# A sample's outer product behind the next block's low parts, in a one-core retention stage

## The chip, the cores and the metric

The kernel runs on one core of one Trainium2 chip. The metric is device microseconds of the whole program on that core; each time is the median of several runs. The engines are named PE (TensorE, matrix products), DVE (VectorE), ACT (ScalarE), POOL (GpSimd) and SP (SyncE, which only issues transfers here). Each engine works through its own queue of instructions in order, and waits in that queue for semaphores that other engines raise.

## What is computed

The reference is one inference step of a two-layer decoder for 1024 new tokens and for 8 running samples of one token each: layer 1 is sliding-window attention and a ConvFFN, layer 2 is retention and a ConvFFN. The change touches the retention layer alone. What matters of it:

```
def step(s, inp):                      # one chunk of 128 tokens, one head
    inner = (q k^T) * decay_in
    o = inner v + (q s) * q_decay
    s = s * chunk_decay + (k * k_decay)^T v
    return s, o
...
mixer over the prompt:  s0 = 0, chunks of 128     (4 heads, keys 256 wide, values 512 wide)
mixer over the samples: s0 = state_ret, chunks of 1
out = (silu(g) * normalised o) @ w_o
```

For a sample the chunk is one token, so per head its state is decayed, gets the outer product of its key and its value, is multiplied by its query, and is written out. All products are float32.

## The kernel before

Every float32 operand of a product is split into a high and a low part, and each product is made as three PE products (high by high, low by high, high by low). ACT writes the high parts (names ending in h) and DVE or POOL subtracts them for the low parts (names ending in l). So weights go from a slab `raw` to `wh` (ACT, L1431) and `wl` (DVE, L2084), a block's keys to `r_kdh` (ACT, L1899) and `r_kdl` (DVE, L2722), its values to `r_vh` and `r_vl`, the state to `r_sh` (ACT, L1969) and `r_sl` (POOL, L3099).

The retention stage is written as `period(i)` for i = 0 to 33, one function of that name for each engine, so that each engine's order is the order of the lines of its own `period`. The 32 blocks are 4 heads times 8 chunks of 128 tokens (n is the chunk in its head); periods 32 and 33 only finish work. In PE's `period` stand, in order: fill 0, `inner` (L1315, keys times queries, waits for r_kdl), `back` of the block before, `update` 0, fill 1, `update` 1 (L792 with r_vh and r_kdh, the state's increment; it waits until DVE has taken update 0's increment into r_state, L2745), fill 2, `output` (the products with r_sh and r_sl), `turn` of the next block (transposes), fill 3, `sample_out`, fill 4. The fills are halves of jobs of the projection that makes the last head's operands (periods 0 to 15, two jobs each; jobs of kinds 1 and 3 are rotated on DVE, L2615, tile p_prod, the others copied on ACT, L1786, tile p_plain), and from 16 on four or five jobs of the output projection, whose results DVE adds to y (L2114). They keep PE busy while the other engines split and normalise.

DVE's `period` has, in order: `decayed` (r_inn, L2727), `gated` (r_ob), `update` 0 into r_state, `inner_lo`, fill 1, `update` 1, sums and masks of the samples, the first planned weight split, `outer`, fill 2, `norm`, `rows` of the next block (r_vl and r_kdl), split 2, fill 3, split 3, fill 4, split 4. The planned splits are a table: in block 12, for example, the third (with wh on ACT and wl on DVE at the same places); from block 16 on also the second.

Beside each block one state of a sample is worked through: SP loads the state (`sample_state`, r_s, 512 KB) and the sample's value row (`sample_values`, r_vb), ACT decays the state (`decay`, L1929), DVE adds the outer product (`outer`, L2755, two instructions of 128 x 512, both inputs in SBUF), PE multiplies it (`sample_out`, L1362), ACT writes it to memory (`sample_state_out`, L1941). Two states fit at a time. At the end `sample_back` (L1370) turns the samples' result.

Before period 0, ACT ends its `ret_pairs` with four plain copies of projection jobs (`LEAD` = 4, p_plain), each of which also issues a transfer; then come `queries_hi(0)` and `values_hi(0)` (r_qkh, r_vh, r_kdh of block 0).

```
dve.wait_ge(R["decay"], i + 1)
dve.wait_ge(R["vb"], 16 * i + 16)
for j in range(2):
    dve.scalar_tensor_tensor(K.s0[:, i % 2, j, :], K.vb[:, :], K.k16[:, j, i % NB:i % NB + 1], K.s0[:, i % 2, j, :],
                             ALU.mult, ALU.add).then_inc(R["outer"], 1)
```

Of the kernel before, what the change touches and what calls it, by code (L numbers as in the profile page):

```python
# [25 lines left out]
RH = 4  # L26
# [14 lines left out]
NI = RH * NB  # L41
# [81 lines left out]
LEAD = 4  # L123


def last_head_jobs():

    return ([(j, ch) for ch in range(NCH) for j in range(4, 8)] + [(2 * p + e, ch) for p in range(2) for ch in range(NCH) for e in range(2)]
            + [(j, ch) for j in (8, 9) for ch in range(NCH)] + [(j, ch) for ch in range(NCH) for j in (10, 11)])
# [668 lines left out]
def tensor_engine(pe, K):  # L798
# [486 lines left out]
    def fill(i, s):  # L1285

        if i < MIXED:
            if s < 4:
                ret_half(FILL[i][s // 2 * 2 + 1][0], s % 2)
            return  # L1290
        for key in FILL[i][s]:
            ret_out(key)
# [34 lines left out]
    def update(i, j):  # L1327
        pe.wait_ge(R["k_lo"], i + 1)
        pe.wait_ge(R["v_lo"], i + 1)
        after(pe, R["state"], 2 * i + j)  # L1330
        kk = slice(j * W, (j + 1) * W)
        accumulate(pe, kvB[:, :], [(K.kdh[:, kk], K.kdl[:, kk], K.vh[:, :], K.vl[:, :])]).then_inc(R["kv"], 1)
# [40 lines left out]
    def period(i):  # L1373
        h, n = divmod(i, NB)
        live = i < NI
        fill(i, 0)
        if live:
            inner(i)
        if 1 <= i <= NI:
            back(i - 1)  # L1380
        if live:
            update(i, 0)
        fill(i, 1)
        if live:
            update(i, 1)
            if n == 0:
                rows(h)
        if i in SAMPLES_BACK:
            sample_back(SAMPLES_BACK.index(i))
        fill(i, 2)  # L1390
        if live:
            output(i)
        if i + 1 < NI:
            turn(i + 1)
        fill(i, 3)
        if 1 <= i <= NI:
            sample_out(i - 1)
        fill(i, 4)

    for g in range(NG):  # L1400
# [9 lines left out]
def scalar_engine(act, K):  # L1410
# [468 lines left out]
    def ret_pairs(u):  # L1879
        ret_batch(u)  # L1880
        ffn_pair(RET, BATCH)
        for t in range(BATCH + 1, END_T[RET]):
            ret_pair(t)
        act.wait_ge(S["hq0"], START["hq0"] + out_count(END_T[RET] - 2))
        for j, ch in last_head_jobs()[:LEAD]:
            project(RH - 1, j, ch)
        for e in range(2):
            act.wait_ge(S[f"hp{e}"], START[f"hp{e}"] + 16 * PAIR_BASE[1] // 2)
# [86 lines left out]
    def fill(jobs):  # L1975
        for key in jobs:
            if key[0] == "p":
                project(*key[1:])

    def period(i):  # L1980
        h, n = divmod(i, NB)
        live = i < NI
        fill(FILL[i][0])
        if live:
            inner_hi(i)
        if 1 <= i <= NI:
            gated_out(i - 1)
        if n == 1 and h:
            sample_parts(h - 1)
        if i == NI + 1:  # L1990
            sample_root(RH - 1)
        fill(FILL[i][1])
        if live:
            decay(i)
            if n == 0:
                sample_rows(h)
        if i in HEADS_SPLIT[:-1]:
            heads_hi(HEADS_SPLIT.index(i))
        if i < NI:
            split_planned(i, 1)  # L2000
        elif FILL[i][1]:
            split_upto(J[FILL[i][1][-1]], U_F1)
        fill(FILL[i][2])
        if 1 <= i <= NI:
            sample_state_out(i - 1)
        if n == 2 and h and live:
            sample_root(h - 1)
        if i in SAMPLES_PUT:
            sample_put(SAMPLES_PUT.index(i))
        if i == HEADS_SPLIT[-1]:  # L2010
            heads_hi(len(HEADS_SPLIT) - 1)
        if live and n == NB - 1:
            state_out(h)
        if i + 1 < NI:
            queries_hi(i + 1)
        if live:
            heads_root(i)
        if i + 1 < NI:
            values_hi(i + 1)
        if live and n < NB - 1:  # L2020
            state_hi(i)
        if MIXED <= i < NI:
            split_planned(i, 2)
        fill(FILL[i][3])
        if i < NI:
            split_planned(i, 3)
        fill(FILL[i][4])
        if i < NI:
            split_planned(i, 4)
        elif FILL[i][4]:  # L2030
            split_upto(J[FILL[i][4][-1]], U_F1)
        if i == NI + 1:
            split_upto(J[FILL[i][3][-1]], U_F1 + 2)
# [13 lines left out]
    ret_pairs(3)  # L2047
    queries_hi(0)
    values_hi(0)
    for i in range(NI + 2):  # L2050
        period(i)
    last_chunks(6)
# [18 lines left out]
def vector_engine(dve, K):  # L2071
# [763 lines left out]
    def period(i):  # L2835
        h, n = divmod(i, NB)
        live = i < NI
        if i == NI + 1:
            sample_sums(RH - 1)
            sample_norm(RH - 1)  # L2840
        fill(FILL[i][0])
        if live:
            decayed(i)
        if 1 <= i <= NI:
            gated(i - 1)
        if live:
            update(i, 0)
            inner_lo(i)
        if i == NI + 1:
            sample_norm_rest(RH - 1)  # L2850
        fill(FILL[i][1])
        if live:
            update(i, 1)
        if n == 1 and live:
            if h:
                sample_sums(h - 1)
            masks(h)
        if n == 2 and h and live:
            sample_norm(h - 1)
        if i < NI:  # L2860
            split_planned(i, 1)
        elif FILL[i][1]:
            split_upto(J[FILL[i][1][-1]], U_F1)
        if 1 <= i <= NI:
            outer(i - 1)
        if i in SAMPLES_BACK:
            sample_gated(SAMPLES_BACK.index(i))
        fill(FILL[i][2])
        if n == 2 and h and live:
            sample_norm_rest(h - 1)  # L2870
        if live:
            norm(i)
        if i in SAMPLES_PUT:
            sample_put(SAMPLES_PUT.index(i))
        if i == NI + 1:
            last_heads_lo()
        if live:
            norm_rest(i)
        if i + 1 < NI:
            rows(i + 1)  # L2880
        if MIXED <= i < NI:
            split_planned(i, 2)
        fill(FILL[i][3])
        if i < NI:
            split_planned(i, 3)
        fill(FILL[i][4])
        if i < NI:
            split_planned(i, 4)
        elif FILL[i][4]:
            split_upto(J[FILL[i][4][-1]], U_F1)  # L2890
        if i == NI + 1:
            split_upto(J[FILL[i][3][-1]], U_F1 + 2)
# [272 lines left out]
def sync_engine(sp, K):  # L3165
# [193 lines left out]
    def period(i):  # L3359
        h, n = divmod(i, NB)  # L3360
        live = i < NI
        if i == 16:
            sp.wait_ge(S["jobs"], J["p", 3, 11, 2])
            heads(0, 2)
        if 1 <= i <= NI:
            slabs_to(planned_slabs(i - 1, 4) + RAW)
        elif i:
            slabs_to(min(due_by(J[(FILL[i - 1][4] or FILL[i - 1][3])[-1]]), S_F1) + RAW)
        if live:
            gates(i)  # L3370
        if i == 14:
            heads_written(8)
            sp.wait_ge(S["jobs"], J["p", 3, 11, 0])
            heads(0, 0)
        if n == 3 and h + 1 < RH:
            decays(h + 1)
        if i < NI:
            slabs_to(planned_slabs(i, 1) + RAW)
        elif FILL[i][1]:
            slabs_to(min(due_by(J[FILL[i][1][-1]]), S_F1) + RAW)  # L3380
        if i in (18, 19, 20):
            heads_written(16)
            heads_landed(i - 18, 1)
            heads(1, i - 18)
        if i == 23:
            heads_written(16 + 3)
            sp.wait_ge(S["jobs"], J["o", 0, 23])
            heads_landed(0, 2)
            heads(2, 0)
        if i == 25:  # L3390
            heads_written(16 + 6)
            heads_landed(1, 2)
            heads(2, 1)
        if i == 26:
            heads_written(24)
            heads_landed(2, 2)
            heads(2, 2)
        if i == 30:
            heads_written(24 + 3)
            sp.wait_ge(S["jobs"], J["o", 1, 23])  # L3400
            heads_landed(0, 3)
            heads(3, 0)
        if i == 31:
            heads_written(24 + 6)
            heads_landed(1, 3)
            heads(3, 1)
        if i == 33:
            heads_written(NI)
            heads_landed(2, 3)
            heads(3, 2)  # L3410
        if i + 1 < NI:
            sample_state(i + 1)
        if live:
            sample_values(i)
        if i == 15:
            sp.wait_ge(S["jobs"], J["p", 3, 11, 1])
            heads(0, 1)
        if i + 2 < NI:
            queries(i + 2)
            values(i + 2)  # L3420
# [206 lines left out]
```

## Time and profile before

| | us |
|---|---|
| median of 3 runs | 2732.18 (2731.06 to 2734.85) |
| the profiled execution | 2737.35 |
| its span in the trace | 2735.3 |
| PE busy in the span | 2665.0 (97%) |
| DVE busy | 1780.3 (65%) |
| ACT busy | 1095.6 (40%) |
| POOL busy | 764.1 (28%) |

The span is what the trace shows from the first instruction to the last; the execution's own time is 2 us longer. The retention blocks run from about 1484 to 1973 us of the span. Busy times are sums over an engine's instructions, so that a wait shows as the rest. In a row of the timeline, the bracket at the end gives how long the engine had been idle before the instruction, and what ended that.

### The profile page before, as it was taken

The page shows a single profiled execution, that of the slowest core. Times are in us where ns is not written, and L with a number is a line of the kernel's source. Part 1 is how long each engine was busy: PE and PEld are TensorE (multiplying, and loading weights), DVE is VectorE, ACT ScalarE, POOL GpSimd, SP SyncE. Part 2 cuts the span into 40 slices and gives each one's busy share as a digit, 9 for nine tenths or more (in the row PEclk, how much of TensorE's full clock was granted, in tenths as well). Part 3 has the DMA queues.
Part 4 walks back from the last instruction along what each step waited for, and adds up shares of the span by engine and source line. Part 5 has one row for each costly group of instructions (what it writes and reads, how often), then busy time and mean ns, then how long its engine had stood idle before and what let it go on. Part 6 is the DMA issues. An engine that isn't in the chain of part 4 may idle for free.

```text
span 2735.3 us, 48829 instructions
## 1 busy us (share of the span) xinstructions
PE 2665.0 (97%) x19550; PEld 2554.2 (93%) x19550; DVE 1780.3 (65%) x3272; ACT 1095.6 (40%) x2089; POOL 764.1 (28%) x601
## 2 busy tenths in 40 slices
PE   8999989999999999999999999999999999999997
PEld 7888879999999999999999888898899999999997
DVE  6556579676667445766463675777787766766455
ACT  5445446434433122633333435433264344342123
POOL 3344351322320002354250232333342223220021
PEclk9999999999999999999999999999999999999999
DMA  4210101222224232122324777776602221223321
GB/s 141 82 47 12 40 33 47 78 86 78 71 91 157 63 123 65 62 98 103 115 94 166 221 226 226 235 227 192 188 25 70 86 78 70 89 94 125 112 73 62
DMA packets 182576, 290.83 MB, mean 106 GB/s; under 512 B 24976, under 2 KB 131088, under 8 KB 182320
## 3 DMA queue, kind: packets, MB, share of 16 engines
q1 hardware_dynamic: 152112, 251.65, 28.4%
q10 hardware_dynamic: 30240, 36.07, 3.7%
q8 instruction: 156, 2.56, 0.4%
q14 instruction: 68, 0.56, 0.1%
HBM read 206.82 MB, written 82.93 MB: 106 GB/s over the span
## 4 chain that ended last, share of the span: by engine, by line
PE 84%; DVE 7%; issue 3%; ACT 2%; DMA 2%; POOL 2%; ACTq 0%; SPq 0%; POOLq 0%; DVEq 0%
PE bank L1085 13%; PE bank L1087 13%; PE bank L1086 13%; PE bank L792 12%; PE bank L794 12%; PE bank L793 12%; PE bank L825 2%; PE bank L827 2%; PE bank L826 2%; PE bank L946 1%; PE bank L925 1%; DVE r_s L2755 1%; DVE wl L2084 1%; ACT wh L1431 1%; PE bank L936 1%
## 5 line engine op out<-in xcount | busy, mean ns | idle before, releaser
L2084 DVE TENSOR_TENSOR wl<-raw,wh 128x512 fp32r<-128x512 f32 (+1 forms) x460 | 428.1, 934 | 310.5 <-ACT wh L1431 307.3
L1431 ACT ACTIVATE wh<-raw 128x512 fp32r<-128x512 f32 (+1 forms) x492 | 344.2, 714 | 405.8 <-PE bank L794 220.8
L1085 PE MATMUL bank<-xh,wh 128*128 128x258 f32 x1792 | 506.2, 283 | 0.0
L1087 PE MATMUL bank<-xh,wl 128*128 128x258 f32 x1792 | 505.7, 282 | 0.0
L1086 PE MATMUL bank<-xl,wh 128*128 128x258 f32 x1792 | 505.0, 282 | 0.0
L1086 PEld LDWEIGHTS bank<-xl,wh 128*128 128x128 f32 x1792 | 338.4, 189 | 0.0
L1085 PEld LDWEIGHTS bank<-xh,wh 128*128 128x128 f32 x1792 | 337.9, 189 | 0.0
L1087 PEld LDWEIGHTS bank<-xh,wl 128*128 128x128 f32 x1792 | 337.6, 188 | 0.0
L2116 DVE TENSOR_TENSOR y<-bank,y 128x344 f32<-128x344 f32 x384 | 191.7, 512 | 213.4 <-PE bank L794 212.5
L3034 POOL TENSOR_TENSOR raw<-raw 128x512 f32<-128x512 f32 x56 | 72.1, 1288 | 742.8 <-DVE wl L2084 742.5
L1085 PE MATMUL bank<-x_t2h,wh 128*128 128x258 f32 x896 | 253.1, 283 | 2.0 <-ACT f_ab L1658 2.0
L1086 PE MATMUL bank<-x_t2l,wh 128*128 128x258 f32 x896 | 253.0, 282 | 0.0
L1087 PE MATMUL bank<-x_t2h,wl 128*128 128x258 f32 x896 | 252.5, 282 | 0.0
L1658 ACT ACTIVATE f_ab<-bank 128x258 f32<-128x258 f32 x224 | 86.3, 386 | 270.7 <-PE bank L1087 267.9
L1085 PEld LDWEIGHTS bank<-x_t2h,wh 128*128 128x128 f32 x896 | 168.9, 189 | 2.3 <-DVE wl L2084 2.3
L1087 PEld LDWEIGHTS bank<-x_t2h,wl 128*128 128x128 f32 x896 | 169.3, 189 | 0.0
L1086 PEld LDWEIGHTS bank<-x_t2l,wh 128*128 128x128 f32 x896 | 169.2, 189 | 0.0
L792 PE MATMUL bank<-xh,wh 128*128 128x344 f32 x488 | 162.7, 333 | 2.4 <-DVE f_cv L2395 1.5
L825 PE MATMUL bank<-xh,wh 128*128 128x344 f32 x472 | 156.9, 332 | 2.6 <-DVE xl L2153 2.3
L794 PE MATMUL bank<-xh,wl 128*128 128x344 f32 x488 | 156.9, 321 | 0.0
L793 PE MATMUL bank<-xl,wh 128*128 128x344 f32 x488 | 156.8, 321 | 0.0
L1658 ACT ACTIVATE f_g<-bank 128x258 f32<-128x258 f32 x224 | 84.3, 380 | 179.4 <-PE bank L1087 179.4
(309 smaller groups left out, 7195.4 us busy)
## 6 DMA issues: line engine op xcount, KB each, us to landing
raw<-in_w SPq DMA_DIRECT2D x216, 512.0 KB, 3.8
scratch_h<-f_g SPq DMA_DIRECT2D x40, 516.0 KB, 2.7
h_in<-scratch_h SPq DMA_DIRECT2D x30, 688.0 KB, 5.0
r_s<-in_state_in SPq DMA_DIRECT2D x32, 512.0 KB, 3.8
out_state_s<-r_s ACTq DMA_DIRECT2D x32, 512.0 KB, 3.5
scratch_qkvg<-f_ab SPq DMA_DIRECT2D x16, 516.0 KB, 4.5
scratch_qkvg<-f_g SPq DMA_DIRECT2D x16, 516.0 KB, 5.5
r_cxq<-scratch_qkvg SPq DMA_DIRECT2D x32, 256.0 KB, 5.3
```

The source lines that it names most:

```text
L792: pe.matmul(out, ah, bh, start=(k == 0), stop=False)
L793: pe.matmul(out, ah, bl, start=False, stop=False)
L794: mm = pe.matmul(out, al, bh, start=False, stop=(k == n - 1))
L825: pe.matmul(out, ah, xh[:, k, c], start=(k == 0), stop=False)
L1085: pe.matmul(out, hi[:, kk], bh, start=(k == 0 and not adds), stop=False, skip_group_check=adds)
L1086: pe.matmul(out, hi[:, kk], bl, start=False, stop=False, skip_group_check=adds)
L1087: mm = pe.matmul(out, lo[:, kk], bh, start=False, stop=(k == 3), skip_group_check=adds)
L1431: act.activation(hi, source, ACT.Copy).then_inc(S["hi_done"], 1)
L1658: act.activation(out, bank[PRODUCT_BANKS[sub][n]][:, 0:TQ], ACT.Copy).then_inc(S[f"copied{sub}"], 1)
L2084: dve.tensor_tensor(lo, source, hi.bitcast(F32), ALU.subtract).then_inc(S["lo_done"], 1)
L2116: dve.tensor_tensor(t, bank[b][:, 0:CH], t, ALU.add).then_inc(S["yadd"], 1)
L3034: pool.tensor_tensor(g[:, two], g[:, one], g[:, two], ALU.add).then_inc(S["w_sum"], 1)
```

## The change

It moves work; nothing is computed otherwise.

- DVE: `outer` of the block before goes from the middle of the period (ahead of fill 2 and `norm`) to behind `rows` of the next block, ahead of split 2 and fill 3; with it the sums and masks of a head's samples.
- PE: `sample_out` goes from between fill 3 and fill 4 to the next period, behind fill 1 and ahead of `update` 1.
- ACT: `decay` is that of the block before; `sample_state_out` goes from ahead of `queries_hi` to behind fill 3, ahead of the third planned split; `sample_parts` goes behind `decay` and `sample_rows`. Two of the four lead copies go behind `values_hi(0)`.
- SP: a sample's value row is loaded after `gates` of the next period, its state in its own period.
- The last head's `sample_sums` on DVE comes behind fill 0 of period 33.

```
--- before.py
+++ after.py
@@ -1380,7 +1380,11 @@
             back(i - 1)
         if live:
             update(i, 0)
+        if i == NI + 1:
+            sample_out(i - 2)
         fill(i, 1)
+        if 2 <= i <= NI:
+            sample_out(i - 2)
         if live:
             update(i, 1)
             if n == 0:
@@ -1393,8 +1397,6 @@
         if i + 1 < NI:
             turn(i + 1)
         fill(i, 3)
-        if 1 <= i <= NI:
-            sample_out(i - 1)
         fill(i, 4)
 
     for g in range(NG):
@@ -1882,7 +1884,7 @@
         for t in range(BATCH + 1, END_T[RET]):
             ret_pair(t)
         act.wait_ge(S["hq0"], START["hq0"] + out_count(END_T[RET] - 2))
-        for j, ch in last_head_jobs()[:LEAD]:
+        for j, ch in last_head_jobs()[:2]:
             project(RH - 1, j, ch)
         for e in range(2):
             act.wait_ge(S[f"hp{e}"], START[f"hp{e}"] + 16 * PAIR_BASE[1] // 2)
@@ -1985,15 +1987,16 @@
             inner_hi(i)
         if 1 <= i <= NI:
             gated_out(i - 1)
-        if n == 1 and h:
-            sample_parts(h - 1)
         if i == NI + 1:
+            sample_parts(RH - 1)
             sample_root(RH - 1)
         fill(FILL[i][1])
-        if live:
-            decay(i)
-            if n == 0:
-                sample_rows(h)
+        if 1 <= i <= NI:
+            decay(i - 1)
+        if live and n == 0:
+            sample_rows(h)
+        if n == 1 and h and live:
+            sample_parts(h - 1)
         if i in HEADS_SPLIT[:-1]:
             heads_hi(HEADS_SPLIT.index(i))
         if i < NI:
@@ -2001,8 +2004,6 @@
         elif FILL[i][1]:
             split_upto(J[FILL[i][1][-1]], U_F1)
         fill(FILL[i][2])
-        if 1 <= i <= NI:
-            sample_state_out(i - 1)
         if n == 2 and h and live:
             sample_root(h - 1)
         if i in SAMPLES_PUT:
@@ -2022,6 +2023,8 @@
         if MIXED <= i < NI:
             split_planned(i, 2)
         fill(FILL[i][3])
+        if 1 <= i <= NI:
+            sample_state_out(i - 1)
         if i < NI:
             split_planned(i, 3)
         fill(FILL[i][4])
@@ -2047,6 +2050,8 @@
     ret_pairs(3)
     queries_hi(0)
     values_hi(0)
+    for j, ch in last_head_jobs()[2:LEAD]:
+        project(RH - 1, j, ch)
     for i in range(NI + 2):
         period(i)
     last_chunks(6)
@@ -2835,10 +2840,10 @@
     def period(i):
         h, n = divmod(i, NB)
         live = i < NI
+        fill(FILL[i][0])
         if i == NI + 1:
             sample_sums(RH - 1)
             sample_norm(RH - 1)
-        fill(FILL[i][0])
         if live:
             decayed(i)
         if 1 <= i <= NI:
@@ -2851,18 +2856,12 @@
         fill(FILL[i][1])
         if live:
             update(i, 1)
-        if n == 1 and live:
-            if h:
-                sample_sums(h - 1)
-            masks(h)
         if n == 2 and h and live:
             sample_norm(h - 1)
         if i < NI:
             split_planned(i, 1)
         elif FILL[i][1]:
             split_upto(J[FILL[i][1][-1]], U_F1)
-        if 1 <= i <= NI:
-            outer(i - 1)
         if i in SAMPLES_BACK:
             sample_gated(SAMPLES_BACK.index(i))
         fill(FILL[i][2])
@@ -2878,6 +2877,12 @@
             norm_rest(i)
         if i + 1 < NI:
             rows(i + 1)
+        if n == 1 and live:
+            if h:
+                sample_sums(h - 1)
+            masks(h)
+        if 1 <= i <= NI:
+            outer(i - 1)
         if MIXED <= i < NI:
             split_planned(i, 2)
         fill(FILL[i][3])
@@ -3368,6 +3373,8 @@
             slabs_to(min(due_by(J[(FILL[i - 1][4] or FILL[i - 1][3])[-1]]), S_F1) + RAW)
         if live:
             gates(i)
+        if 1 <= i <= NI:
+            sample_values(i - 1)
         if i == 14:
             heads_written(8)
             sp.wait_ge(S["jobs"], J["p", 3, 11, 0])
@@ -3408,10 +3415,8 @@
             heads_written(NI)
             heads_landed(2, 3)
             heads(3, 2)
-        if i + 1 < NI:
-            sample_state(i + 1)
-        if live:
-            sample_values(i)
+        if 1 <= i < NI:
+            sample_state(i)
         if i == 15:
             sp.wait_ge(S["jobs"], J["p", 3, 11, 1])
             heads(0, 1)
```

DVE's queue, from update 1 of block 12 to the start of block 13 (r_s is the sample's state, bank a PSUM bank), before:

```order
L2745 SCALAR_TENSOR_TENSOR r_state<-r_state,r_dec,bank 128x512
L2755 SCALAR_TENSOR_TENSOR r_s_145<-r_vb,r_k_156,r_s_145 128x512 x2
L2771 BN_STATS r_st_139<-bank 128x6
...
L2720 TENSOR_TENSOR r_vl<-bank,r_vh 128x512
L2722 SCALAR_TENSOR_TENSOR r_kdl<-bank,r_dec,r_kdh 128x256
L2084 TENSOR_TENSOR wl<-raw,wh 128x1024
L2727 TENSOR_TENSOR r_inn<-bank,r_dec 128x128
```

and after (lines are shifted by five):

```order
L2725 TENSOR_TENSOR r_vl<-bank,r_vh 128x512
L2727 SCALAR_TENSOR_TENSOR r_kdl<-bank,r_dec,r_kdh 128x256
L2760 SCALAR_TENSOR_TENSOR r_s_145<-r_vb,r_k_156,r_s_145 128x512 x2
L2089 TENSOR_TENSOR wl<-raw,wh 128x1024
L2732 TENSOR_TENSOR r_inn<-bank,r_dec 128x128
L2742 TENSOR_TENSOR r_ob<-bank,r_cxg 128x512
L2750 SCALAR_TENSOR_TENSOR r_state<-r_state,r_dec,bank 128x512
```

The outer product now stands between the low parts and the weight split, ahead of r_inn and of the r_state that PE's update 1 waits for.

ACT's queue at the same place, from the sample's decay in block 12, before:

```order
L1929 ACTIVATE r_s_145<-r_s_145,r_dec 128x1024
L1941 DMA out_state_s<-r_s_145 128x1024
L1905 ACTIVATE r_qkh<-r_cxq 128x256
...
L1969 ACTIVATE r_sh<-r_state 128x1024
L1786 ACT_TABLE_LOAD
L1786 ACTIVATE p_plain<-bank 128x344
L1788 DMA scratch_qkvg<-p_plain 128x344
L1431 ACTIVATE wh<-raw 128x1024
```

and after:

```order
L1931 ACTIVATE r_s_145<-r_s_145,r_dec 128x1024
L1907 ACTIVATE r_qkh<-r_cxq 128x256
...
L1971 ACTIVATE r_sh<-r_state 128x1024
L1788 ACT_TABLE_LOAD
L1788 ACTIVATE p_plain<-bank 128x344
L1790 DMA scratch_qkvg<-p_plain 128x344
L1943 DMA out_state_s<-r_s_145 128x1024
L1433 ACTIVATE wh<-raw 128x1024
```

The store of the sample's state, which waits for the outer product, now stands directly ahead of the weight split.

## Rows read from the trace of the kernel before

**Rows 1.** Windows: stretch, us, busy us and instructions by engine, clock, DMA share, GB/s

```profile
1484.00:1973.00 489.00, 467.35 (x2940) 418.70 (x2939) 340.40 (x654) 197.81 (x331) 149.51 (x99) 0.98 0.70 218
1494.00:1501.00 7.00, 5.91 (x21) 5.58 (x22) 2.22 (x5) 0.61 (x3) 0.14 (x1) 0.54 0.16 61
1722.00:1726.00 4.00, 4.00 (x17) 3.71 (x16) 2.89 (x5) 1.37 (x2) 0.00 (x0) 0.57 0.93 264
```

The engines stand in the order PE, PE's weight loads, DVE, ACT, POOL.

**Rows 2.** Waits of PE, 1484 to 1973: total us, times, longest us

```profile
PE bank L1315 <- DVE r_kdl L2722: 9.9, 4, 3.6
PE bank L792 <- DVE r_state L2745: 6.0, 5, 1.7
...
PE bank L1362 <- DVE r_s L2755: 1.3, 1, 1.3
```

**Rows 3.** Timeline, block 0 and the start of block 16: start, us, instruction [idle before]

```profile
1485.49 0.60 PE L1309 MATMUL bank<-ident,r_cxv 128*128 128x128 f32 x4
...
1490.70 0.46 ACT L1786 ACTIVATE p_plain<-bank 128x344 f32<-128x344 f32 x1 [6.64 <-DMA scratch_qkvg<-p_plain]
...
1495.09 1.22 PE L1315 MATMUL bank<-r_cxq 128*128 128x128 f32 x4 [3.35 <-DVE r_kdl L2722]
...
1721.27 0.71 PE L1315 MATMUL bank<-r_cxq 128*128 128x128 f32 x4 [2.41 <-DVE r_kdl L2722]
```

**Rows 4.** Timeline, end of block 5 and block 6 up to update 1

```profile
1571.14 0.39 PE L794 MATMUL bank<-r_sh,r_qkl 128*128 128x512 f32 x1
...
1574.78 0.47 DVE L2722 SCALAR_TENSOR_TENSOR r_kdl<-bank,r_dec,r_kdh 128x256 fp32r<-128x256 f32 x1
1574.85 2.40 POOL L3099 TENSOR_TENSOR r_sl<-r_state,r_sh 128x1024 fp32r<-128x1024 f32 x1 [1.99 <-ACT r_sh L1969]
...
1575.17 0.51 DVE L2615 TENSOR_TENSOR p_prod<-bank,cosR 128x344 f32<-128x344 f32 x1
...
1576.44 0.51 DVE L2615 TENSOR_TENSOR p_prod<-bank,sinR 128x344 f32<-128x344 f32 x1
...
1580.02 0.39 PE L792 MATMUL bank<-r_vh,r_kdh 128*128 128x512 f32 x1
```

**Rows 5.** Timeline, DVE and POOL where both subtract or add SBUF tiles

```profile
1582.75 1.41 DVE L2755 SCALAR_TENSOR_TENSOR r_s<-r_vb,r_k,r_s 128x512 f32<-128x512 f32 x2
...
1710.49 4.32 POOL L3107 TENSOR_TENSOR xl<-xl,xh 128x688 fp32r<-128x688 f32 x2 [5.16 <-ACT xh L1920]
...
1713.20 2.82 DVE L2755 SCALAR_TENSOR_TENSOR r_s<-r_vb,r_k,r_s 128x512 f32<-128x512 f32 x2
...
1764.52 2.38 POOL L3099 TENSOR_TENSOR r_sl<-r_state,r_sh 128x1024 fp32r<-128x1024 f32 x1 [2.58 <-ACT r_sh L1969]
...
1765.41 2.56 DVE L2084 TENSOR_TENSOR wl<-raw,wh 128x1024 fp32r<-128x1024 f32 x1 [0.50 <-ACT wh L1431]
```

**Rows 6.** Timeline, block 12 from the sample's store to update 1 of block 13

```profile
1669.07 0.34 ACTq L1941 DMA_DIRECT2D out_state_s<-r_s  x1
...
1674.70 0.47 DVE L2722 SCALAR_TENSOR_TENSOR r_kdl<-bank,r_dec,r_kdh 128x256 fp32r<-128x256 f32 x1
...
1676.92 1.06 ACT L1431 ACTIVATE wh<-raw 128x1024 fp32r<-128x1024 f32 x1 [0.46 <-ACT p_plain L1786]
...
1678.01 1.23 DVE L2084 TENSOR_TENSOR wl<-raw,wh 128x1024 fp32r<-128x1024 f32 x1 [2.84 <-ACT wh L1431]
...
1680.83 0.47 PE L792 MATMUL bank<-r_vh,r_kdh 128*128 128x512 f32 x1 [1.32 <-DVE r_state L2745]
```

**Rows 7.** Timeline, an addition of the output filler, block 17

```profile
1735.45 0.51 DVE L2114 SCALAR_TENSOR_TENSOR y<-y,bank 128x344 f32<-128x344 f32 x1 [0.47 <-PE bank L794]
```

**Rows 8.** Timeline, PE's last sample product and the turn of the samples' result

```profile
1964.16 0.62 PE L1362 MATMUL bank<-r_s,r_qm 128*8 128x256 f32 x8
...
1968.42 0.31 PE L794 MATMUL bank<-xh,wl 128*128 128x344 f32 x1
1970.35 0.41 PE L1370 MATMUL bank<-ident,r_xv 8*128 8x8 f32 x4 [1.61 <-DVE r_xv L2805]
```

More of the change, by code:

```diff
@@ L1382, in period @@
             update(i, 0)
+        if i == NI + 1:
+            sample_out(i - 2)
         fill(i, 1)
+        if 2 <= i <= NI:
+            sample_out(i - 2)
         if live:
@@ L1395, in period @@
         fill(i, 3)
-        if 1 <= i <= NI:
-            sample_out(i - 1)
         fill(i, 4)
@@ L1884, in ret_pairs @@
         act.wait_ge(S["hq0"], START["hq0"] + out_count(END_T[RET] - 2))
-        for j, ch in last_head_jobs()[:LEAD]:
+        for j, ch in last_head_jobs()[:2]:
             project(RH - 1, j, ch)
@@ L1987, in period @@
             gated_out(i - 1)
-        if n == 1 and h:
-            sample_parts(h - 1)
         if i == NI + 1:
+            sample_parts(RH - 1)
             sample_root(RH - 1)
         fill(FILL[i][1])
[L1993 to L1996, printed above, removed]
+        if 1 <= i <= NI:
+            decay(i - 1)
+        if live and n == 0:
+            sample_rows(h)
+        if n == 1 and h and live:
+            sample_parts(h - 1)
         if i in HEADS_SPLIT[:-1]:
@@ L2003, in period @@
         fill(FILL[i][2])
-        if 1 <= i <= NI:
-            sample_state_out(i - 1)
         if n == 2 and h and live:
@@ L2024, in period @@
         fill(FILL[i][3])
+        if 1 <= i <= NI:
+            sample_state_out(i - 1)
         if i < NI:
@@ L2049, in scalar_engine @@
     values_hi(0)
+    for j, ch in last_head_jobs()[2:LEAD]:
+        project(RH - 1, j, ch)
     for i in range(NI + 2):
@@ L2837, in period @@
         live = i < NI
+        fill(FILL[i][0])
         if i == NI + 1:
@@ L2840, in period @@
             sample_norm(RH - 1)
-        fill(FILL[i][0])
         if live:
@@ L2853, in period @@
             update(i, 1)
[L2854 to L2857, printed above, removed]
         if n == 2 and h and live:
@@ L2863, in period @@
             split_upto(J[FILL[i][1][-1]], U_F1)
-        if 1 <= i <= NI:
-            outer(i - 1)
         if i in SAMPLES_BACK:
@@ L2880, in period @@
             rows(i + 1)
+        if n == 1 and live:
+            if h:
+                sample_sums(h - 1)
+            masks(h)
+        if 1 <= i <= NI:
+            outer(i - 1)
         if MIXED <= i < NI:
@@ L3370, in period @@
             gates(i)
+        if 1 <= i <= NI:
+            sample_values(i - 1)
         if i == 14:
@@ L3410, in period @@
             heads(3, 2)
[L3411 to L3414, printed above, removed]
+        if 1 <= i < NI:
+            sample_state(i)
         if i == 15:
```

## The prediction

> **What bounds the kernel now.** I read the busy time by stretch first: in the retention stage, 1484 to 1973 us, TensorE (PE) is busy 467.35 of 489 us at a mean granted clock of 0.98, and VectorE (DVE), ScalarE (ACT) and GpSimd (POOL) are busy 340, 198 and 150 [rows 1]. So PE is the bound, and a move inside the stage can give back at most the 21.65 us in which PE is idle and what a lower clock costs. Second, PE's waits in that stretch: 9.9 us in four waits for r_kdl (the low part of the scaled keys), 6.0 in five for r_state, 1.3 in one for a sample's r_s [rows 2], and 1.61 at the end for r_xv [rows 8]. Third, the clock: behind the wait of 3.35 us in the first block PE ran from 1494 to 1501 at a mean of 0.54, and from 1722 to 1726 at 0.57 behind the wait of 2.41 for r_kdl that ended at 1721.27; half speed is 1.2 GHz, full 2.4 [rows 1, 3]. Fourth, the timeline of single blocks, for what a wait would be if DVE did something else there.
>
> **First block: a gain.** PE has turned block 0's keys and values by 1485.49 + 0.60 = 1486.09, when ACT could split them, but ACT first waits 6.64 us for a transfer before its third plain copy, at 1490.70, and then makes the fourth; PE's product of keys waits for the result until 1495.09, 3.35 us [rows 3]. The change puts those two copies behind the splits. r_kdl then is ready by about 1488, before PE wants it at 1495.09 − 3.35 = 1491.74. Gain: 3.35, and the low clock behind it, some 5.4 us of busy PE at half speed that take 2.7 less at full. Together **−6.0** (−3.35 if only the wait goes; +0 is rival 4).
>
> **The steady block: where the outer product goes.** In block 5 output ends at 1571.14 + 0.39 = 1571.53, r_kdl at 1574.78 + 0.47 = 1575.25, so 3.72 later, and PE begins update 1 of block 6 at 1580.02, 8.49 us after output's end [rows 4]. PE doesn't wait there: it has 8.49 us of work of its own (fillers, the sample's product, inner, back, update 0), and sample_out's move, 0.62 us [rows 8], stays inside these 8.49. In that time DVE has r_vl, r_kdl, [here the outer product now], the filler's rotation, r_inn, r_ob, r_state; update 1 waits for that r_state. From the last DVE piece before r_inn to update 1 I take 1.59: in block 13 wl ends at 1678.01 + 1.23 = 1679.24 and update 1 starts at 1680.83, released by r_state [rows 6].
>
> **How long is the outer product at the new place?** Alone the pair takes 1.41 us [rows 5]. But at the new place POOL's r_sl (state minus its high part) has just begun: 1574.85, while r_kdl ends at 1575.25, and r_sl lasts 2.40 [rows 4], in each of the 28 blocks in which a head goes on. Where an outer product met a POOL subtraction of two SBUF tiles, it was held: the pair begun at 1713.20 took 2.82 us and ended 1.21 after the POOL pair (1710.49 + 4.32 = 1714.81). The low-part subtraction wl met r_sl itself at 1765.41 and took 2.56 in place of 1.23 [rows 5, 6]; its end, 1767.97, is 1.07 behind r_sl's 1766.90. POOL was never lengthened. All ten outer products that overlapped such a POOL instruction in the trace and all seven wl that overlapped r_sl were held. So I price the new place at 2.00 until r_sl ends, and 1.21 more: done 3.72 + 2.00 + 1.21 = 6.93 behind output's end. The chain is 6.93 + 1.59 = 8.52 against PE's 8.49: a plain block loses nothing, but **nothing is left over**. Everything that DVE has between outer product and r_inn becomes a wait of PE. Bounds: 1.41 (not held) and 3.21.
>
> What lies there, block by block:
> - Blocks with a rotation at the last filler (5, 6, 7, 9): four products from 1575.17 at 0.42, 1.69 us [rows 4]; before, they were done before r_sl ended. 4 × 1.72 = 6.9.
> - Weight splits. The sample's store on ACT now stands ahead of the split, and it waits for the outer product; so wh waits too. Then 0.42 (the store's issue), 1.06 (wh), 1.23 (wl) [rows 6], 2.7 us in all. Before, wh started right behind a plain copy at 1676.92, with the store far ahead, at 1669.07 [rows 6]. Block 13, whose split is written in block 12, shows the working: r_kdl ends at 1674.70 + 0.47 = 1675.17, and 2.00 + 1.21 + 2.7 + 1.59 later it is 1682.7; PE was ready at 1680.83 − 1.32 = 1679.51 [rows 6], so it waits 3.2. In the same way blocks 3 and 4 wait 2.8 each, 10 4.0 (a rotation and a sample's sums on top), 11 3.1 and 1.9 more at inner, 13 3.2, 16 2.4, 20 1.3 (its split stands behind the last filler), 29 3.2, together 24.7.
> - y additions of the output filler, up to 0.51 each [rows 7], two take about 0.9: 1.4 in block 17, 0.9 in 21, 23 and 25, together 4.1. Odd blocks from 17 on have a fifth filler, which covers the rest.
> - Splits that came ahead of the filler on DVE (blocks 18, 26, 30; the next update 1 waits): 1.23 behind the outer product and two y additions, about 2.05 each: 6.1.
> - Smaller remainders in blocks 2, 12, 14, 15, 18 and 26: 3.1.
>
> Sum of new waits: 6.9 + 24.7 + 4.1 + 6.1 + 3.1 = **+44.9**. I worked each block out from its own rows; those shown are the pattern, and one block may be off by 0.5.
>
> **What goes away.** The waits of before in these places: r_kdl without the first block 9.9 − 3.35 = 6.55, r_state 6.0, r_s 1.3 [rows 2], **−13.9**: they are replaced by the ones above, and r_kdl's, which came of sums and outer products ahead of r_vl, mostly vanish. With two of them go two stretches of half clock (the one at 1722 in rows 1 and one of equal length behind the longest wait of rows 2), some 3.4 us each at half speed, so 1.7 each: **−3.4**.
>
> **The clock behind the new waits.** Seven of the new waits are 2.7 us or more, as long as those that were followed by half speed (2.41 to 3.6), though two lie near others; I count six places and take four at 1.7: **+6.8** (0 to 12).
>
> **The end.** sample_out of the last sample moves from 1964.16 to behind one more filler; between that product's end at 1964.78 and 1968.73 PE does two, so one is 2.0 [rows 8]. What follows from it, sample_back at 1970.35, already waits 1.61, and so waits as much longer: **+1.9** (0 if r_xv comes of something else).
>
> **At nothing.** ACT's decay moves a block later at the same place, beside PE. SP's sample loads move by half a block: the sample's rows now wait for the outer product before, at the block's start; behind them in SP's queue stand weight slabs for a block later. Their cover is about 7 us; if it were gone, one split would start late, and I put that at up to 3 us in all.
>
> **Sum.** 44.9 + 6.8 + 1.9 − 13.9 − 3.4 − 6.0 = +30.3 us. The profiled execution took 2737.35, the median of the runs 2732.18; the sum is of differences, so I lay it on the median: 2732.2 + 30.3 = **2762.5**.
>
> **Rivals.** (1) Faster: the outer product isn't held. r_kdl and r_sl are only 0.40 us apart, and no row shows an outer product against r_sl. If DVE got in first, or if the two don't exclude one another, the chain is 3.72 + 1.41 + 1.59 = 6.72 and 1.8 us of cover remain in each block; rotations fit, splits cost about 1 each, and new waits of about 12 are left without a low clock: 12 + 1.9 − 13.9 − 3.4 − 6.0 = −9, so **2723**. It decides from the point where DVE's start comes ahead of r_sl's. Against it: in rows 4 and 6 r_sl starts before r_kdl ends, both behind ACT's r_sh and r_kdh, whose order the change leaves. The Trainium skill (SBUF — State Buffer, "SBUF: two separate sides") says that a DVE instruction with two SBUF inputs and a GpSimd instruction that reads SBUF exclude each other for the whole instruction, and that whichever starts first keeps the ports. By that rule the held outer product and wl above are what must happen, the trace agrees with 17 of 17, and with DVE first it would be POOL that is held, about 1.4 us, which costs nothing here, since r_sl is wanted only at the next output.
> (2) Half the price: PE's cover isn't 8.49 everywhere, or stores come earlier because the queue has slack; new waits are 25 and two half clocks: 25 + 3.4 + 1.9 − 23.3 = +7 to +15, **2744**.
> (3) The clock falls behind every wait over 2 us, twelve of them: 20 in place of 6.8, +43: **2775**.
> (4) The first block's gain doesn't come, because something else waits for the two plain copies: +6: 2768.5, inside the forecast's range.
>
> **Chances.** Forecast (with 4) 0.60, rival 1 0.13, rival 2 0.17, rival 3 0.10. The range takes in rival 2, most of 3, and leaves rival 1: 2733 to 2778. About 0.2% (5.5 us) is what a measurement can tell from no change: faster 0.14 (rival 1 and a bit), same 0.08 (the low end of rival 2), slower 0.78.
>
> **What would show it.** PE's waits for r_kdl in the first block gone; r_s (outer) instructions starting at r_kdl's end and lasting 3.2 the pair, ending 1.21 behind r_sl; PE's waits for r_state some 45 us in about twenty places, the longest (3 and more) in blocks 10, 11, 13 and 29; ACT's wh in those blocks behind the store; PE busy in the stage unchanged but for the clock. It is wrong if the outer pair there takes 1.4, or if the waits for r_state stay near 6.

## The result and the profile after

The changed kernel takes 2767.39 us, the median of 4 runs (2765.45 to 2770.2), beside 2733.27 (2731.06 to 2734.85) for the kernel before: a ratio of 1.0119, with a 95% interval of 1.0107 to 1.0131. The ratios here and below are those on record; the quotient of two medians can differ from them in the fourth place (here 1.0125). By the medians that is 34.1 us slower; 30.3 had been forecast, from the median then known. Lines of the new code are five further on than before in DVE's and POOL's part and two in ACT's.

The page of the changed kernel first gives the span, then the busy time of each engine:

```profile
span 2768.4 us, 48828 instructions
## 1 busy us (share of the span) xinstructions
PE 2674.7 (97%) x19550; PEld 2565.0 (93%) x19550; DVE 1805.4 (65%) x3272; ACT 1097.0 (40%) x2089; POOL 760.0 (27%) x601
```

The same 97% for PE says nothing. The stretch does: one of the retention stage with the same 2940 PE instructions as the first of [rows 1], one of the first block, and one behind a long wait (stretch, its us, then busy us of PE, weight loads, DVE, ACT and POOL; clock; DMA):

```profile
1484.00:2006.60 522.60, 477.31 (x2940) 429.21 (x2939) 364.85 (x654) 198.60 (x331) 145.52 (x99) 0.96 0.64 204
1494.00:1501.00 7.00, 7.00 (x47) 6.50 (x46) 2.43 (x7) 3.70 (x8) 0.73 (x1) 1.00 0.32 96
1698.00:1706.00 8.00, 6.19 (x20) 5.70 (x21) 2.62 (x6) 1.92 (x3) 0.00 (x0) 0.57 0.82 245
```

The stage is 33.6 us longer (522.6 against 489.0). PE's idle time in it went from 21.65 to 45.29, that is +23.6; its busy time from 467.35 to 477.31, +10.0, for the same instructions at a mean clock of 0.96 in place of 0.98. The first block is healed: 7.00 us busy of 7 at full clock, where it had been 5.91 at 0.54.

The waits of PE in the stage (total us, times, longest), to be laid beside [rows 2]:

```profile
PE bank L792 <- DVE r_state L2750: 39.4, 22, 3.7
PE bank L1370 <- DVE r_xv L2810: 2.5, 1, 2.5
PE bank L792 <- DVE r_state L2754: 1.8, 1, 1.8
PE bank L792 <- DVE y L2121: 0.5, 1, 0.5
PE bank L792 <- DVE y L2119: 0.5, 1, 0.5
PE bank L1362 <- DVE r_s L2760: 0.3, 1, 0.3
```

No row for r_kdl is left (9.9 before). In its place stands r_state at update 1, in 22 blocks by the first row and in block 16 by the third.

The clock, stretch by stretch (columns as in the stage's row above): behind the wait of 2.89 us in block 3 it stays at full speed, as the first row shows; the other nine are the stretches of the stage at half speed, at the waits of blocks 4, 6, 7, 10, 11, 13, 16, 19 and 29:

```profile
1533.00:1549.50 16.50, 13.61 (x93) 11.97 (x85) 11.32 (x17) 7.03 (x12) 3.12 (x2) 1.00 0.76 241
1551.66:1558.49 6.83, 6.11 (x18) 5.61 (x19) 1.53 (x3) 1.15 (x1) 0.00 (x0) 0.50 0.93 291
1585.80:1589.21 3.41, 3.41 (x13) 3.21 (x12) 1.76 (x2) 2.10 (x2) 0.00 (x0) 0.50 0.52 176
1602.86:1606.28 3.42, 3.42 (x14) 3.42 (x13) 0.75 (x1) 0.99 (x1) 0.00 (x0) 0.50 0.99 253
1647.24:1654.07 6.83, 5.82 (x18) 5.37 (x19) 3.85 (x8) 4.86 (x5) 1.05 (x2) 0.50 0.88 269
1667.72:1671.13 3.41, 3.41 (x15) 3.01 (x14) 2.07 (x3) 2.05 (x2) 0.00 (x0) 0.50 0.98 304
1698.44:1705.26 6.82, 5.45 (x17) 5.09 (x18) 2.18 (x4) 1.92 (x3) 0.00 (x0) 0.50 0.85 245
1746.22:1749.64 3.42, 3.42 (x14) 3.06 (x13) 0.69 (x1) 2.01 (x4) 0.40 (x1) 0.50 1.05 387
1794.01:1797.42 3.41, 3.41 (x13) 3.31 (x12) 0.59 (x2) 0.54 (x2) 3.09 (x2) 0.50 1.02 292
1947.61:1951.02 3.41, 3.41 (x13) 3.31 (x12) 1.88 (x2) 1.20 (x2) 0.00 (x0) 0.50 0.87 286
```

That is 41 us at half speed, in which PE is busy 37.9; the kernel before had 13.6 in three stretches. One more begins at the very end of the stage in both kernels.

The timeline around block 13's update shows the whole chain (start, us, engine, instruction, idle before it and what ended that):

```profile
1691.76 0.48 DVE L2727 SCALAR_TENSOR_TENSOR r_kdl<-bank,r_dec,r_kdh 128x256 fp32r<-128x256 f32 x1
1691.83 2.38 POOL L3104 TENSOR_TENSOR r_sl<-r_state,r_sh 128x1024 fp32r<-128x1024 f32 x1 [2.57 <-ACT r_sh L1971]
1692.16 3.27 DVE L2760 SCALAR_TENSOR_TENSOR r_s<-r_vb,r_k,r_s 128x512 f32<-128x512 f32 x2
...
1695.45 0.34 ACTq L1943 DMA_DIRECT2D out_state_s<-r_s  x1
1695.90 1.06 ACT L1433 ACTIVATE wh<-raw 128x1024 fp32r<-128x1024 f32 x1 [2.37 <-DVE r_s L2760]
1696.99 1.23 DVE L2089 TENSOR_TENSOR wl<-raw,wh 128x1024 fp32r<-128x1024 f32 x1 [1.57 <-ACT wh L1433]
...
1699.81 0.77 PE L792 MATMUL bank<-r_vh,r_kdh 128*128 128x512 f32 x1 [3.24 <-DVE r_state L2750]
```

The outer pair starts at r_kdl's end, 0.33 behind POOL's r_sl, and takes 3.27 us in place of 1.41; it ends at 1695.43, 1.22 behind r_sl's end at 1694.21. The store on ACT waits for it, wh for the store, wl for wh, update 1 for what follows. 3.24 us of wait were forecast as 3.2.

The 64 outer products in the groups of instructions, first of the kernel before (busy us, mean ns of one):

```profile
L2755 DVE SCALAR_TENSOR_TENSOR r_s<-r_vb,r_k,r_s 128x512 f32<-128x512 f32 x64 | 61.1, 995 | 0.2
```

In the changed kernel:

```profile
L2760 DVE SCALAR_TENSOR_TENSOR r_s<-r_vb,r_k,r_s 128x512 f32<-128x512 f32 x64 | 89.5, 1438 | 0.3 <-DMA r_vb<-scratch_rows 0.2
```

### The profile page after: what moved, and what is told of

Its sections match the earlier page's. It is cut to its first block, busy times and chain, and to the rows that moved or that the text cites. A ratio compares the mean times of both kernels' runs of the same rounds, so it can differ in the third digit from the quotient of the medians.

```text
span 2768.4 us, 48828 instructions
## 1 busy us (share of the span) xinstructions
PE 2674.7 (97%) x19550; PEld 2565.0 (93%) x19550; DVE 1805.4 (65%) x3272; ACT 1097.0 (40%) x2089; POOL 760.0 (27%) x601
## 4 chain that ended last, share of the span: by engine, by line
PE 82%; DVE 9%; issue 3%; ACT 3%; POOL 2%; DMA 0%; ACTq 0%; SPq 0%; DVEq 0%; POOLq 0%
PE bank L1085 13%; PE bank L1087 13%; PE bank L1086 13%; PE bank L792 12%; PE bank L794 11%; PE bank L793 11%; PE bank L825 2%; PE bank L826 2%; PE bank L827 2%; DVE r_s L2760 1%; POOL r_sl L3104 1%; PE bank L946 1%; PE bank L925 1%; DVE r_state L2750 1%; ACT wh L1433 1%
## 5 line engine op out<-in xcount | busy, mean ns | idle before, releaser
L2089 DVE TENSOR_TENSOR wl<-raw,wh 128x512 fp32r<-128x512 f32 (+1 forms) x460 | 421.6, 920 | 307.5 <-ACT wh L1433 305.5
```

The lines of the kernel that those rows point to most:

```text
L2089: dve.tensor_tensor(lo, source, hi.bitcast(F32), ALU.subtract).then_inc(S["lo_done"], 1)
```

## The experiments

**The lead copies alone.** The kernel before, with only this part of the change:

```
-        for j, ch in last_head_jobs()[:LEAD]:
+        for j, ch in last_head_jobs()[:2]:
...
     values_hi(0)
+    for j, ch in last_head_jobs()[2:LEAD]:
+        project(RH - 1, j, ch)
```

> The kernel before with one part of the change alone: two of ACT's four lead copies go behind the splits of the first block. Theory: PE's wait for r_kdl at the first block (3.35 us) and the half clock behind it go, 6.0 us: 2727.3 us, with the clock at 1.0 from 1494 to 1501 us and the other waits as before. Rival (the two copies make something else late, their transfers or the filler's banks): the wait comes back at another line of the first two blocks, 2732 to 2734 us.

Measured: 2730.66 us beside 2734.15, a ratio of 0.9988 (0.9979 to 0.9997), 3.5 us with an interval of 0.8 to 5.7. The first block's stretch is whole:

```profile
1494.00:1501.00 7.00, 7.00 (x46) 6.29 (x45) 2.79 (x7) 5.10 (x9) 0.74 (x1) 1.00 0.31 109
```

So the cause holds and the gain is real, but under the 6.0 expected, which lies outside that interval. In the two profiled executions the time from the first block's turn to the samples' turn at the stage's end fell by 4.9: of PE's idle time the 3.35 of the first block went, and 0.7 came back in other waits.

**The outer product back, all else as changed.**

```
             update(i, 1)
+        if n == 1 and live:
+            if h:
+                sample_sums(h - 1)
+            masks(h)
...
+        if 1 <= i <= NI:
+            outer(i - 1)
         if i in SAMPLES_BACK:
...
             rows(i + 1)
-        if n == 1 and live:
-            if h:
-                sample_sums(h - 1)
-            masks(h)
-        if 1 <= i <= NI:
-            outer(i - 1)
```

> The changed kernel with the outer products (and a head's sums and masks) back in the middle of DVE's period, all else as changed. Theory (the place of the outer product behind r_kdl, where r_sl holds it, is what costs): outer pairs take 1.41 us, the 22 waits for r_state (39.4 us) fall to about 6, the waits for r_kdl of before in the later blocks (6.6 us) come back, the first block's gain and the later end stay: 2729 us, 2725 to 2735. Rival A (ACT's store ahead of the weight split costs, wherever the outer product is): the waits of the blocks with a split (3, 4, 10, 11, 13, 29, of 2.9 to 3.7 us) stay, 2750 us or more. Rival B (PE's moved sample product or SP's later loads cost): waits for r_s or for the sample's loads appear, 2745 us or more.

Measured: 2746.97 us, a ratio of 1.0044 (1.0029 to 1.0060). The theory was half right: r_state's waits fell to 5.7 us with ACT's store still ahead of the split, so the split blocks' waits had come of the late outer product, and rival A is out. But the time missed 2729 by 18 us, and rival B had named the place. The wait of DVE at the outer product, in this kernel:

```profile
DVE r_s L2760 <- DMA r_vb<-scratch_rows: 26.8, 12, 4.5
```

And PE's waits for the keys' low part, in the same kernel:

```profile
PE bank L1315 <- DVE r_kdl L2727: 16.0, 8, 3.6
```

The sample's value row, now loaded at the period's start, lands too late for an early outer product; DVE stands there, and norm and r_kdl queue behind it. The late place had hidden that load. The two edits lean on each other.

**The value row back as well.** The same kernel, with SP's `sample_values(i)` again behind `sample_state` at the end of the period.

> The changed kernel with the outer products, sums and masks in the middle of DVE's period again, and also the load of the sample's value row at its old place at the end of SP's period. In the run with the outer products alone put back, DVE stood 26.8 us (12 times) at the outer product for r_vb, and PE 16.0 us for r_kdl. Theory (that was the price of loading the value row at the period's start when the outer product is early): the waits for r_vb vanish, r_kdl's fall from 16.0 to about 6.4 as before, and the time comes to 2729 to 2734 us, near that of the kernel with the lead copies alone. Rival (ACT's or PE's part of the change keeps DVE late): r_vb's waits go but 10 us or more of r_kdl's stay, 2742 us or more.

Measured: 2729.3 us beside 2735.28, a ratio of 0.9977 (0.9967 to 0.9988). DVE's waits for r_vb are gone, and PE's for r_kdl are 6.5 us in four. With the outer products and their rows where they had been, the rest of the change (lead copies, PE's sample product, ACT's decay and store) costs nothing. Whether it is worth anything beyond the lead copies stays open, since the intervals of the two kernels overlap.

**POOL's r_sl behind the outer product.** The changed kernel, and in POOL's `state_lo`:

```
         pool.wait_ge(R["s_hi"], rows_of_state(i) + 1)
+        if i:
+            pool.wait_ge(R["outer"], 2 * i)
```

> The changed kernel with one wait added on POOL: its r_sl (state minus high part) starts only when the outer product of that period is done. Theory (r_sl holds the outer product): outer pairs take 1.41 us again at the same place, the rotation blocks' waits of 1.75 us vanish, the split blocks' fall by about 1 us (wl then meets r_sl), the sum of waits for r_state goes from 39 to 15 to 20 us and half of the half clock goes: 2738 us, 2730 to 2746. Rival (the outer product is long at this place by itself, or PE's wait comes of something else): the pair stays at 3.27 us, r_sl only ends later, 2767 us or more.

Measured: 2740.53 us, a ratio of 1.0019 (1.0010 to 1.0028). One added wait on another engine takes back 27 of the 34 us, at the outer product's new place. The group of outer products in this kernel:

```profile
L2760 DVE SCALAR_TENSOR_TENSOR r_s<-r_vb,r_k,r_s 128x512 f32<-128x512 f32 x64 | 46.9, 774 | 0.2
```

And PE's waits at update 1:

```profile
PE bank L792 <- DVE r_state L2750: 20.9, 20, 3.0
```

The outer products take 774 ns each on the mean, where it had been 1438: r_sl is what held them. PE's waits for r_state came out just above what was expected (15 to 20). The rotation blocks' waits of 1.74 to 1.77 us fell to 0.15 to 0.50.

**The store behind the split.** The changed kernel, and on ACT:

```
         fill(FILL[i][3])
-        if 1 <= i <= NI:
-            sample_state_out(i - 1)
         if i < NI:
             split_planned(i, 3)
+        if 1 <= i <= NI:
+            sample_state_out(i - 1)
```

> The changed kernel with the sample's store on ACT behind the third planned weight split in place of ahead of it. Theory: wh is ready when the outer product ends, so wl follows it at once; the waits of update 1 in blocks 3, 4, 10, 11, 13, 16 and 29 fall by 1.5 us each (3.2 to 1.7), and three or four half-clock stretches go: 2767.4 - 10.5 - 4 = 2753 us, 2749 to 2758; the rotation blocks keep their 1.75. Rival A (ACT's stall is the whole cost of those blocks): their waits vanish, 2740 to 2746 us. Rival B (the store's place is worth nothing, DVE's queue alone sets the wait): 2765 to 2769 us.

Measured: 2749.13 us, a ratio of 1.0055 (1.0041 to 1.0068), 18.3 us less than the changed kernel. Update 1 of blocks 3 and 13, in this kernel:

```profile
1532.30 0.47 PE L792 MATMUL bank<-r_vh,r_kdh 128*128 128x512 f32 x1 [1.22 <-DVE r_state L2750]
...
1683.14 0.47 PE L792 MATMUL bank<-r_vh,r_kdh 128*128 128x512 f32 x1 [1.57 <-DVE r_state L2750]
```

2.89 and 3.24 became 1.22 and 1.57, as the theory had it; blocks 16 and 29 fell by only 1.05 and 1.23, and block 10 kept 3.70: there a rotation of 1.7 us stands on DVE between outer product and split, and ACT's store and wh were done beside it before. The waits for r_state fell from 39.4 to 31.5, by 8. The larger part came of the clock: 13.6 us of the stage at half speed are left of 41. The stretch from block 2 to block 9, in this kernel (columns as above):

```profile
1518.00:1632.00 114.00, 104.56 (x670) 94.44 (x669) 84.23 (x146) 38.58 (x67) 31.58 (x25) 1.00 0.69 213
```

The same blocks in the changed one:

```profile
1518.00:1640.00 122.00, 108.66 (x661) 97.54 (x660) 83.04 (x146) 38.41 (x68) 29.82 (x25) 0.94 0.64 201
```

The rotation blocks have waits of 1.74 us and more in both; where the split blocks ahead of them had shrunk to 1.2, none was followed by half clock.

**Both repairs.** The changed kernel with r_sl behind the outer product and the store behind the split.

> The changed kernel with both repairs: the store behind the third planned split on ACT, and POOL's r_sl behind the outer product. Theory (whichever of the DVE and the POOL instruction starts first holds the other): wl stands right behind the outer product with its wh long ready, so it begins before POOL has seen the outer product's end, takes 1.23 us, and r_sl ends later instead; the split blocks' waits of 1.8 to 2.2 us fall below 0.7, PE's waits for r_state come to 8 to 12 us, and no half clock is left before block 10: 2727 us, 2722 to 2732. Rival (POOL gets in first after the outer product): wl takes 2.4 us or more there, the split blocks keep about 2 us of wait: 2737 to 2742 us.

Measured: 2732.95 us, a ratio of 0.9993 (0.9983 to 1.0003), just above the theory's range: both theory and rival happened, in different blocks. PE's waits for r_state were 19.2 us, where the theory had 8 to 12; no half clock before block 10 was left, as it had said. First block 2 with wl first, then block 12 with r_sl first:

```profile
1529.55 1.23 DVE L2089 TENSOR_TENSOR wl<-raw,wh 128x1024 fp32r<-128x1024 f32 x1
1529.60 3.42 POOL L3106 TENSOR_TENSOR r_sl<-r_state,r_sh 128x1024 fp32r<-128x1024 f32 x1 [3.87 <-DVE r_s L2760]
...
1533.12 0.75 DVE L2750 SCALAR_TENSOR_TENSOR r_state<-r_state,r_dec,bank 128x512 f32<-128x512 f32 x1 [1.55 <-POOL r_sl L3106]
...
1675.25 2.40 POOL L3106 TENSOR_TENSOR r_sl<-r_state,r_sh 128x1024 fp32r<-128x1024 f32 x1 [4.45 <-DVE r_s L2760]
...
1676.62 2.11 DVE L2089 TENSOR_TENSOR wl<-raw,wh 128x1024 fp32r<-128x1024 f32 x1 [1.52 <-ACT wh L1433]
```

With wl 0.05 us ahead, wl takes its 1.23 and r_sl takes 3.42 in place of 2.40: now POOL is held. And the time returns at r_state, which may not overwrite the state before r_sl has read it, 1.55 us: the blocks behind such a split wait 1.17. In block 12 a table load and a plain copy stand ahead of wh on ACT, r_sl is first, wl is held (2.11), and block 13 waits 2.21 as it did without the store's move.

**Idle products in the waits.** The changed kernel; on PE, ahead of update 1 in 14 blocks, 10 to 25 transposes into a PSUM bank that nobody reads then:

```
+        for _ in range({3: 19, 4: 18, 5: 10, 6: 10, 7: 10, 9: 10, 10: 25, 11: 19, 13: 21, 16: 10, 19: 12, 27: 14, 29: 22, 31: 13}.get(i, 0)):
+            pe.transpose(uB[:, 0:W], ident[:, :], ident[:, :])
         if live:
             update(i, 1)
```

> The changed kernel with idle products on PE: in the 14 blocks that wait over 1.7 us for r_state, 10 to 25 transposes of the identity into an unused PSUM bank, ahead of update 1, so that PE is busy for most of the wait and waits 0.3 to 0.8 us behind them. Nothing that is computed changes. Theory (PE's half clock comes of its standing idle in those waits, and costs 10 us in the stage beyond the waits themselves): the clock stays at 1.0 from 1500 us to the end of the stage, and the time falls by 8 to 11 us though PE has more to do: 2757 us, 2755 to 2760. Rival A (the low clock comes with what the other engines do, or with the waits' number): as many half-clock stretches, 2767 us or more. Rival B (the clock cost less than the trace's busy time says): the stretches go and the time stays within 2 us of 2767.

Measured: 2753.42 us, a ratio of 1.0066 (1.0051 to 1.0081): 14.0 us less than the changed kernel (16.0 if each is laid beside its own runs of the kernel before), with 213 PE instructions more. The stage in this kernel:

```profile
1484.00:1991.10 507.10, 485.62 (x3155) 436.21 (x3154) 364.49 (x654) 198.37 (x330) 145.62 (x99) 1.00 0.66 210
```

And the timeline of PE at block 13, the transposes and update 1:

```profile
1688.07 2.51 PE L1389 MATMUL bank<-ident 128*128 128x128 f32 x21
...
1691.40 0.47 PE L792 MATMUL bank<-r_vh,r_kdh 128*128 128x512 f32 x1 [0.81 <-DVE r_state L2752]
```

The clock is 1.00 throughout, and the stage is 15.5 us shorter than the changed kernel's (507.1 against 522.6). That is the clock: PE's busy time without the 213 transposes (26.32 us) is 459.30, which is 18.0 less than the changed kernel's 477.31, while its idle time and the transposes together are 47.80 us, where 45.29 were idle. The gain is above the 8 to 11 expected: those had been read from the difference of busy times, which leaves out what the half clock had cost before the change, 6.1 by the prediction's own terms (3.4 and 2.7).

**The late place where it pays.** The kernel with early outer products and late value rows, but the late place in one or two periods, and the store behind the third split:

```
+        if 1 <= i <= NI and i not in (10, 15):
             outer(i - 1)
...
             rows(i + 1)
+        if i in (10, 15):
+            outer(i - 1)
```

> The kernel with the early outer products and the late value row (2729.3 us), with the outer product behind the low parts in two periods alone, 10 and 15, and the store behind the third split in all. Those are the periods in which the early outer product makes PE wait for the next block's keys: 2.78 us at block 11, behind a sample's sums, and 2.65 at block 16, where POOL's xl holds the pair for 3.31 us. Theory (which place costs less depends on what shares the ports there): those two waits and the 0.83 and 1.24 at update 1 become about 1.2 at block 11 and 0.7 at block 16, a half-clock stretch goes: 5 to 7 us less, 2723 us, 2721 to 2726. Rival (the value row of the next sample then comes late, as it did with the early load, since it waits for the late outer product): new waits for r_vb of 2 to 4 us in periods 11 and 16 make blocks 12 and 17 wait, 2728 to 2733 us.

> As the kernel with periods 10 and 15, but period 15 alone has the late outer product. Theory: only block 16's 2.65 and 1.24 us become about 0.7: 3 us less than 2729.3 us, so 2726 us, 2724 to 2729. Rival (a late value row in period 16): 2729 to 2732 us.

Measured: 2725.53 us with both periods, a ratio of 0.9968 (0.9955 to 0.9980) to the kernel before, and 2726.55 with period 15 alone, 0.9972 (0.9960 to 0.9983). Both lie in their expected ranges and below the kernel before and the changed one. But they can't be told apart from each other, nor from the kernel with all outer products early (0.9977, 0.9967 to 0.9988), so that the late place pays in these periods isn't shown by the times. And the store's move is in both: with period 15 alone, block 13, which lies ahead of that period, already went from 1.81 to 1.33 us and lost the half clock behind it. What the late place did shows in the traces: block 16 waits 0.74 and 0.75 in place of 2.65 and 1.24. One new wait took 1.7 and 1.6 of it back, for a transfer; with both periods:

```profile
PE bank L1307 <- DMA r_cxq<-scratch_qkvg: 1.7, 1, 1.7
```

No wait of DVE for r_vb appeared, so the rival's place was wrong. But the value row did come late, since it waits for the outer product, and r_cxq's load stands behind it in SP's queue: counted from the r_cxg load before them, both go out 2.2 us later than with the early outer product. PE, which no longer waits so long at block 16, also reaches that place sooner; what part each has in the 1.7 us isn't shown.

## Why the prediction was right, point by point

- **The place** was right: the outer pair takes 3.27 (3.21 forecast), r_sl holds it, and the chain of 8.52 us against PE's 8.49 leaves nothing. The pair takes 3.26 to 3.29 in 22 of 32 cases; eight take 1.4, where a head ends and there is no r_sl, or where a head's sums or masks stand between. The four blocks without anything behind the outer product (2, 12, 14 and 15) wait 0.45 to 0.60 us, which the prediction has among its smaller remainders (3.1; with blocks 18 and 26 they measure 2.98). That r_sl holds the pair was an inference from other pairs of instructions; the run with r_sl put behind it shows it.
- **The prices by block** were right: rotation blocks 1.74 to 1.77 each (1.72 forecast), blocks 3 and 4 2.89 and 2.85 (2.8), 13 3.24 (3.2), 29 3.27 (3.2), 20 1.42 (1.3), 21, 23 and 25 0.90 to 0.91 (0.9), 19, 27 and 31 2.07, 2.21 and 2.08 (2.05). Too high were 10 (3.71 against 4.0), 11 (2.86 against 3.1), 16 (1.79 against 2.4), 17 (1.11 against 1.4) and the 1.9 at block 11's inner, which didn't come. Waits of update 1 sum to 42.2, with the two for y; 44.9 had been forecast, with that 1.9.
- **What goes away**: 13.9 were forecast, with 3.35 in the first block. The r_kdl waits all went; also 2.3 us for r_xo and for issue that the sum had left out. So PE's idle time grew by 23.6, where the terms give 44.9 + 1.9 − 13.9 − 3.35 = 29.5.
- **The clock is the term that was mis-sized.** The terms give 6.8 − 3.4 − 2.7 = +0.7; PE's busy time grew by 10.0. The step that failed is "I count six places and take four at 1.7". Nine stretches of the changed stage ran at half speed, among them two at waits of 1.75 us (blocks 6 and 7), one at 1.79 (16) and one at 2.07 (19), which the prediction didn't count; and three of the nine were twice as long as counted. Block 3, one of the long waits (2.89), had none. The idle products show the price, 15.5 us of time and 18.0 of PE's busy time, above the upper bound of 12 given for this term. Rival 3's 20 was nearer, but not its rule: of the nine waits over 2 us at update 1, those of blocks 3, 27 and 31 (2.89, 2.21, 2.08) were not followed by half clock, and three shorter ones were.
- The two errors, 6 us too many in waits and 9 too few in clock, nearly cancel; that the sum came within 4 us of the result is partly luck.
- **The end**: r_xv's wait grew from 1.61 to 2.49, by 0.9, not by 1.9.
- **The first block** was right in cause; alone it is worth 3.5 (0.8 to 5.7) against 6.0.
- **"At nothing"**: loading the value row at the period's start costs nothing beside the late outer product (0.2 us of DVE's wait), as said; with the outer product early it costs 18 us, as two of the runs show.
- **Misread, without harm to the sum**: "POOL was never lengthened". It was, in the trace of the kernel before: every xl that began while a wl or an outer product ran took 1.88 to 2.69 us, the others 1.62 to 1.72 (two rows are in the last section). Nine outer pairs overlap such a POOL instruction there, not ten; all nine are long, but in three (at 1772.05, 1873.56 and 1960.94 us) the first of the two came ahead of POOL's and took its 0.74 or 0.75. Rival 1 takes a held r_sl to cost nothing; in the run with both repairs r_state waits 1.55 us for it.

## What to carry to other kernels

Before a subtraction or a product of two SBUF tiles is moved on DVE, look at what POOL runs at the new place: here the same 1.41 us pair took 3.27, and the queue behind it paid. Where an engine at 97% has its next step fed by a chain of equal length, any step put into that chain is paid in full, so the chain is to be worked out from the rows (8.52 against 8.49 here) before the free time of the engine. Many waits of about 2 to 3 us on PE can cost more than their sum; count the half-clock time with them.

## What the runs showed of the hardware

Of the two xl that [rows 5] gives as one row of 4.32 us, the second alone, in the kernel before, with the wl that DVE had just begun:

```profile
1712.06 1.23 DVE L2084 TENSOR_TENSOR wl<-raw,wh 128x1024 fp32r<-128x1024 f32 x1 [2.89 <-ACT wh L1431]
1712.12 2.69 POOL L3107 TENSOR_TENSOR xl<-xl,xh 128x688 fp32r<-128x688 f32 x1
```

- DVE and POOL hold each other both ways. DVE's wl, 0.05 us ahead, held POOL's r_sl for a microsecond (3.42 in place of 2.40). The kernel before has it too: behind a wl that began 0.06 us before it, xl took 2.69, where the first of the pair took 1.69. The Trainium skill says so (SBUF — State Buffer, "SBUF: two separate sides": whichever starts first keeps the shared ports for its whole instruction); the trace agrees in both directions, and the two started 0.05 and 0.33 us apart.
- In the changed kernel a wait of 1.74 us in block 5 and one of 2.89 in block 3 were not followed by half clock, those of 1.75 in blocks 6 and 7 were, and in the kernel with the store behind the split none of 1.74 to 1.77 was. What decides between them stays open.
- PE kept busy with work that nobody needs made the program 14.0 us faster.
